# Attention outputs copied whole by ScalarE, shifted by DMA and added on GpSimd; keys loaded in column halves

## The reference, cut to what matters

```python
mod = jax.nn.silu(c) @ w_ada + b_ada                       # shift, scale, gate
h = rmsnorm(x, norm_in) * (1.0 + scale[:, None, :]) + shift[:, None, :]
proj = h @ w_in
# per block of 128 queries: index scores pick 256 keys, then
logits = jnp.einsum('bqhd,bqkhd->bqhk', q_b, k_sel) * att_scale
p = jax.nn.softmax(jnp.where(valid, logits, -jnp.inf), axis=-1)
y_attn = jnp.einsum('bqhk,bqkhd->bqhd', p, v_sel)
y_attn = group_rmsnorm(y_attn, gn_attn, N_HEADS) * jax.nn.silu(az)
y = jnp.concatenate([y_conv, y_attn], axis=-1) @ w_out
return rmsnorm(x + gate[:, None, :] * y, norm_f)
```

## Time and profile before

| | |
|---|---|
| Time, median of 3 runs | 688.26 us (688.07 to 688.32) |
| Profiled execution | 688.04 us |
| Its span | 686.2 us |
| PE busy | 654.1 us, 95% |
| DVE busy | 452.2 us, 66% |
| ACT busy | 376.3 us, 55% |
| POOL busy | 229.4 us, 33% |
| Granted TensorE clock | 0.999 of full speed |

### The profile page before, as it was taken

The page is one execution under the profiler, slowest core; times in us unless marked ns, Lnnn a source line. Parts: engine busy times, 40 slices in busy tenths (PEclk is TensorE's granted clock), DMA queues, the critical chain, the costliest instruction groups (busy, mean ns, idle before and its releaser), DMA issues.

```text
span 686.2 us, 8973 instructions
## 1 busy us (share of the span) xinstructions
PE 654.1 (95%) x3203; PEld 547.5 (80%) x3203; DVE 452.2 (66%) x750; ACT 376.3 (55%) x546; POOL 229.4 (33%) x121
## 2 busy tenths in 40 slices
PE   0999999999999999999999999999999999999996
PEld 0889987878888888888888888788788887778884
DVE  4884746767889999996038750003899898577625
ACT  6766444656562232454552453444899999874202
POOL 1001234343334152657645856540026432000000
PEclk9999999999999999999999999999999999999999
DMA  8960496453333011111010361034884551222431
GB/s 314 381 234 1 140 183 138 137 155 94 93 92 122 33 54 40 57 35 61 32 63 31 123 215 61 32 91 94 281 193 112 124 124 39 87 92 97 150 123 61
DMA packets 27911, 78.64 MB, mean 115 GB/s; under 512 B 3986, under 2 KB 8410, under 8 KB 27868
## 3 DMA queue, kind: packets, MB, share of 16 engines
q1 hardware_dynamic: 27524, 77.03, 37.4%
q10 hardware_dynamic: 344, 1.05, 0.6%
HBM read 61.25 MB, written 13.41 MB: 109 GB/s over the span
## 4 chain that ended last, share of the span: by engine, by line
PE 81%; DVE 5%; DMA 4%; ACT 4%; issue 2%; SPq 1%; POOL 1%; ACTq 1%; DVEq 0%; POOLq 0%
PE ps L808 15%; PE ps L810 15%; PE ps L809 15%; PE ps L1018 4%; PE ps L1020 4%; PE ps L1019 4%; PE ps L845 4%; PE ps L878 2%; PE ps L879 2%; PE ps L966 2%; PE ps L965 2%; PE ps L897 2%; PE ps L898 2%; DMA iqs<-hlL 1%; PE ps L698 1%
## 5 line engine op out<-in xcount | busy, mean ns | idle before, releaser
L808 PE MATMUL ps<-hH,wH 128*128 128x512 f32 (+1 forms) x544 | 211.7, 389 | 0.1
L809 PE MATMUL ps<-hL,wH 128*128 128x512 f32 (+1 forms) x544 | 210.1, 386 | 0.0
L810 PE MATMUL ps<-hH,wL 128*128 128x512 f32 (+1 forms) x544 | 210.1, 386 | 0.0
L1857 POOL TENSOR_TENSOR wL<-raw,wH 128x1024 fp32r<-128x1024 f32 x35 | 87.7, 2505 | 183.8 <-ACT wH L1076 175.7
L810 PEld LDWEIGHTS ps<-hH,wL 128*128 128x128 f32 x544 | 102.1, 188 | 20.3
L808 PEld LDWEIGHTS ps<-hH,wH 128*128 128x128 f32 x544 | 102.1, 188 | 20.1 <-issue 1.6
L809 PEld LDWEIGHTS ps<-hL,wH 128*128 128x128 f32 x544 | 102.2, 188 | 18.5
L1278 ACT ACTIVATE relu<-ps,wabs 128x384 f32<-128x384 f32 (+5 forms) x48 | 40.1, 850 | 39.4 <-PE ps L898 14.6
L1581 DVE SCALAR_TENSOR_TENSOR score<-relu,wsgn,score 128x384 f32<-128x384 f32 (+5 forms) x42 | 49.7, 1183 | 13.6 <-ACT relu L1278 10.2
L1602 DVE TENSOR_SCALAR_CACHE_REDUCE above<-score,srch 128x384 bf16<-128x384 f32 (+5 forms) x60 | 56.8, 946 | 2.1
L1697 DVE TENSOR_TENSOR phL<-ps,phH 128x512 fp32r<-128x512 f32 (+1 forms) x80 | 49.3, 632 | 11.6 <-ACT phH L1234 10.7
(11 more groups left out here) (233 smaller groups left out, 1182.2 us busy)
## 6 DMA issues: line engine op xcount, KB each, us to landing
raw<-in_w_units SPq DMA_DIRECT2D x36, 512.0 KB, 3.4
ks<-qk_halves SPq DMA_DIRECT2D x32, 256.0 KB, 5.9
xin<-in_x SPq DMA_DIRECT2D x8, 512.0 KB, 8.0
wa<-in_w_ada SPq DMA_DIRECT2D x8, 512.0 KB, 11.7
wa<-in_w_ada SPq DMA_DIRECT2D x16, 256.0 KB, 7.7
gw<-in_w_ada SPq DMA_DIRECT2D x8, 512.0 KB, 4.1
qs<-qk_halves SPq DMA_DIRECT2D x16, 256.0 KB, 4.2
wo<-in_w_out SPq DMA_DIRECT2D x8, 512.0 KB, 7.7
```

Source lines behind the costliest of these rows:

```text
L808: pe.matmul(out, wH[slot(n)][:, kt, :], hH[:, kt, cols], start=(kt == 0), stop=False)
L809: pe.matmul(out, wH[slot(n)][:, kt, :], hL[:, kt, cols], start=False, stop=False)
L810: mm = pe.matmul(out, wL[slot(n)][:, kt, :], hH[:, kt, cols], start=False, stop=(kt == KT - 1))
L1857: g.tensor_tensor(wL[slot(n)][:], raw[slot(n)][:], wH[slot(n)][:].bitcast(F32), ALU.subtract).then_inc(s_wL, 1)
```

## The change

**Opening.** Tile 1 joins `STAGED`, so only tile 0 is read from PSUM, and the third unit's first matmul no longer waits for `xT` of tile 1.

**Outputs.** For g below `SHIFTED` = 14, ACT copies the whole bank of 128x512, for an even head into its place in `ya`, for an odd one into the new tile `obuf`. The bank is free from then (`out_read` waits for `s_tmp`). SP shifts the half that lies in the wrong rows to `tmp` with a DMA (`shift_out`), and GpSimd adds (`join`). The last head (g = 14, 15) stays as it was.

**Key loads.** `load_head` loads a head in two halves of 512 columns, six DMAs of 64x512 each, with a semaphore for each half; the shifts, the weight rows (four at head 0, two at head 2) and the denominators (heads 1, 3, 5) stand between them. Head 0 and 1 are loaded in four such parts.

**Tables.** New places for logits, maxima, exponentials, outputs, denominators and group sums. One weight row is split by GpSimd in each of the second and third pair, two in the first.

```diff
-STAGED = (2, 3, 4, 5, 6, 7)
+STAGED = (2, 3, 4, 5, 6, 1, 7)
-LOGITS_AT = (1, 3, 10, 13, 14, 15, 16, 18)
-MAX_AT = (1, 2, 9, 14, 14, 15, 15, 18)
-EXP_AT = (9, 13, 13, 16, 16, 17, 19, 21)
+LOGITS_AT = (2, 5, 5, 11, 16, 16, 18, 20)
+MAX_AT = (0, 4, 6, 10, 15, 16, 17, 20)
+EXP_AT = (6, 9, 15, 18, 18, 19, 21, 24)
-TMP_AT, OUT_AT = 5, 5
+TMP_AT, OUT_AT = 4, 5
+SHIFTED = 2 * (NH - 1)
...
+        def kept_out(g):
+            h, sb = g // 2, g % 2
+            return ya[:, h // 2, HALF * sb:HALF * sb + HALF] if h % 2 == 0 else obuf[:]
...
-                        if n:
-                            pe.wait_ge(s_h, n)
+                        if n == 1:
+                            pe.wait_ge(s_h, 1)
...
+            def shift_out(g):
+                sp.wait_ge(s_tmp, g + 1)
+                if g:
+                    sp.wait_ge(s_join, g)
+                r, d = rows(g // 2), rows(g // 2 + 1)
+                sp.dma_start(tmp[r, :], kept_out(g)[d, :]).then_inc(s_shift, 16)
...
-                if g >= 1:
-                    act.wait_ge(s_o, g)
-                A(tmp[r, :], ps[d, 6 + sb, :], ACT.Copy).then_inc(s_tmp, 1)
+                if g < SHIFTED:
+                    if h % 2 and g > 2:
+                        act.wait_ge(s_join, g if sb else g - 2)
+                    A(kept_out(g), ps[:, 6 + sb, :], ACT.Copy).then_inc(s_tmp, 1)
...
-                    if x in OUTS:
+                    if x in OUTS and OUTS[x] >= SHIFTED:
                         head_out(OUTS[x])
...
+            def join(g_):
+                h, sb = g_ // 2, g_ % 2
+                r = rows(h)
+                pool.wait_ge(s_shift, 16 * (g_ + 1))
+                ...
+                g.tensor_tensor(ya[r, h // 2, HALF * sb:HALF * sb + HALF], kept_out(g_)[r, :], tmp[r, :],
+                                ALU.add).then_inc(s_join, 1)
```

More of the change, by code:

```diff
@@ L193 @@
 HEAD = 2 * STEPS
[L194 to L197, removed]
+DSQ_AT = {HEAD * (2 * t + 1) + (4 if t < NT - 1 else 5): t for t in range(NT)}
+DENS_AT = {HEAD * (2 * t + 1) + (9 if t < NT - 1 else 7): t for t in range(NT)}
+KEEP_AT = {HEAD * (2 * t + 1) + (14 if t < NT - 1 else 9): t for t in range(NT)}
+SUMS_AT = {HEAD * (2 * t + 2) + 7 + 8 * half: (t, half) for t in range(NT - 1) for half in range(2)}
 SUMS_AT[LAST + 15] = (NT - 1, 0)
-KEEP_SUMS_AT = {HEAD * (2 * t + 2) + 5 + 8 * half: (t, half) for t in range(NT - 1) for half in range(2)}
+KEEP_SUMS_AT = {HEAD * (2 * t + 2) + 7 + 9 * half: (t, half) for t in range(NT - 1) for half in range(2)}
 OUT_HIGH_AT = {LAST + x: 4 + n for n, x in enumerate((11, 14, 17, 18))}
@@ L330, in build @@
         tmp = at("tmp", [P, HALF], F32, 76)
+        obuf = at("obuf", [P, HALF], F32, 12)
         masked = [at(f"masked{i}", [P, S], F32, kb) for i, kb in enumerate((56, 60))]
@@ L392, in build @@
         s_wo = sem("s_wo"); s_woH = sem("s_woH"); s_woL = sem("s_woL"); s_woLd = sem("s_woLd")
-        s_stack = [sem(f"s_stack{i}") for i in range(2)]
+        s_stack = [sem(f"s_stack{part}") for part in range(2)]
         s_vh = sem("s_vh"); s_vv = sem("s_vv")
@@ L644, in spread_den, with load_head @@
                                  dd[t, NB * e:NB * e + NB, :].rearrange("(o b) n -> o (b n)", o=1).broadcast_to([HD, S])).then_inc(s_din, 16)
-            for h in range(NH):
-                if h == 2:
+            def load_head(h, part):
+                if h == 2 and part == 0:
                     sp.wait_ge(s_unit, NU)
-                if h >= 2:
+                if h >= 2 and part == 0:
                     sp.wait_ge(s_lg, NB * (h - 1))
+                if h:
+                    sp.wait_ge(s_stack[part], 96 * h)
+                cols = slice(HALF * part, HALF * part + HALF)
@@ new lines, in shift_out @@
+            def shift_out(g):
[4 more added lines that the diff above has]
+                sp.dma_start(tmp[r, :], kept_out(g)[d, :]).then_inc(s_shift, 16)
+            for h in range(2):
+                for part in range(2):
+                    load_head(h, part)
+            for h in range(NH):
+                if h:
+                    shift_out(2 * h - 1)
+                if h + 2 < NH:
+                    load_head(h + 2, 0)
+                if h == 0:
+                    load_head(2, 1)
+                if h < NH - 1:
+                    shift_out(2 * h)
+                if h == 0:
+                    for ct in range(4):
+                        sp.dma_start(wo[:, ct, :], a["w_out"][P * ct:P * ct + P, :]).then_inc(s_wo, 16)
+                elif h + 2 < NH:
+                    load_head(h + 2, 1)
@@ L656, in _ @@
                 if h == 2:
-                    for ct in range(KT - 2):
+                    sp.wait_ge(s_wo, 16 * 4)
+                    for ct in range(4, KT - 2):
                         sp.dma_start(wo[:, ct, :], a["w_out"][P * ct:P * ct + P, :]).then_inc(s_wo, 16)
-                if h >= 3 and h % 2:
-                    spread_den((h - 3) // 2)
+                if h % 2 and h < NH - 1:
+                    spread_den(h // 2)
             sp.wait_ge(s_exp, NB * NH)
@@ L1298, in other_half @@
                 act.wait_ge(s_pv, last_chunk(g) + 1)
[L1299 to L1301 removed]
+                if g < SHIFTED:
+                    if h % 2 and g > 2:
+                        act.wait_ge(s_join, g if sb else g - 2)
+                    A(kept_out(g), ps[:, 6 + sb, :], ACT.Copy).then_inc(s_tmp, 1)
+                else:
+                    act.wait_ge(s_join, SHIFTED)
+                    if sb:
+                        act.wait_ge(s_o, 1)
+                    A(tmp[r, :], ps[d, 6 + sb, :], ACT.Copy).then_inc(s_tmp, 1)
             def pair_cols(t, half):
@@ L1943, in pair_add @@
                 pool.wait_ge(s_sums, 2 * t + half + 1)
+                if half == 0:
+                    pool.wait_ge(s_join, 4 * t + 5)
                 pool.wait_ge(s_din, 32 * (t + 1))
```

62 lines of the change are left out of this document (45 added, 17 removed).

## The result

The changed kernel is slower: median 690.97 us (22 runs; 21 lie between 687.66 and 693.51, and the one of 1344.12 us is left out of the ratio) against 688.03 us for the kernel before (22 runs, 686.76 to 689.39). The ratio is 1.0049, 95% interval 1.0041 to 1.0057. I had forecast 686.4 and a range that ended at 689.9. The profiled execution took 693.33 (span 691.4), 2.4 us above the median, so its losses are larger than the typical ones.

A forecast was written before the change was run, and what follows sets the result against it. TensorE, busy 95% of the span, was taken as the bound. Attention stalls of -2.75 us and new waits of +0.9 gave net -1.85, from the median of 688.26 to 686.4 us; range 684.5 to 689.9.

The forecast's parts named there:

- The step that failed: Attention outputs: next shift, group sums and ACT wait for the join; ACT's loop 8.4 us against 9.7, so no wait.
- The landing: Output shift by DMA: lands between 0 and 5.9 us after issue, the upper bound taken from a 256 KB key load.
- VectorE's relief, -2.75: Attention: 14 output adds leave VectorE, 2.7 us less per pair; TensorE stalls shrink by 1.7, 0.3 and 0.75 us.
- Last exponential, +0.9 in heads 1 to 6: Turn of values block 3: a 2.76 us chain against 2.6 of TensorE work, so 0.15 us wait per head.
- VectorE and GpSimd: Attention: VectorE reads PSUM and one SBUF tile, so it is not open to blocking by GpSimd's SBUF reads.
- Opening, 0: Opening: TensorE's 1.69 us wait for tile 1 goes, but it then waits for VectorE's sums; 0, bounds 0 and -1.8.
- GpSimd's join 1.3: Attention outputs: GpSimd's 64x512 add takes 1.3 us, bounds 0.65 and 1.3; no room problem on GpSimd.
- ACT's whole copy 0.59: Attention outputs: ScalarE's 128x512 copy, 0.59 us, replaces a 64x512 one of 0.592; cost 0.
- key halves: Key loads in halves: 6.5 instead of 3.2 us of SP per head; cost 0, bounds 0 and +1.
- tail 0: End of attention: 8.0 us of TensorE work and 1.85 of stalls, before 6.75 and 1.87; 0, bounds -0.5 and +1.

The follow-up runs named there:

- The shift first: Changed kernel with all three denominator broadcasts issued behind the shift of the odd head's second half, not ahead of it: 687.22 us, ratio 0.9989 to the kernel before.
- VectorE's version: Changed kernel with each odd head's second-half output copied across by ScalarE and added by VectorE, as before: 687.34 us, ratio 0.9992; timed again 686.61, 0.9989.
- the kernel with only the first spread moved: Changed kernel with only the first of three denominator broadcasts moved behind the shift (head 2): 695.85 us, ratio 1.0122 to the kernel before.
- the best profile: First profile of the changed kernel with odd heads' second-half outputs added by VectorE: attention stage 100.2 us, against 101.9 in the kernel before.

## Why the prediction was wrong

- **The step that failed.** "Who waits for it: the next shift, the group sums, and ACT". I named the sums and priced only ACT: 9.7 us of window against a loop of 8.4. The sums' wait stands in my sum at nothing, without a reason. Theirs is the longer chain, with a square (1.04) behind the join, up to 9.4, and the shorter window: counted as I counted ACT's it is 11 of a head's 20 places, 7.6 us, and it measured 6.05. That is up to 1.8 us by my own numbers, and up to 3.4 by the measured window, in each of three heads, slower where I said faster. The runs showed 4.1 us of such waits (2.7, 0.7, 0.7). The shift first and VectorE's version show that this chain is all of the loss.
- **The landing.** The bound of 5.9 us held in the changed kernel (2.2 at least, 2.8 in the middle, 5.4 at most; 6.1 once in the kernel with only the first spread moved), and the case of interest, behind two broadcasts of 256 KB, lay at its upper end. The Trainium skill (SBUF — State Buffer, section The DMA setup-cost knee) has a nearly fixed cost of some 2 us per transfer; the shortest landing, 2.2, agrees, and the 5.4 shows what came on top of it with other transfers in flight. "No wait even at the upper bound, if SP is free": SP was free but for 0.28 us at most, the transfers' engines were not (share 0.98; 0.67 and 0.56 where the same shift took 3.6 us in heads 4 and 6).
- **The clock.** No term for it. It cost 1.7 us in one profile of the changed kernel and none in the other.
- **VectorE's relief, -2.75.** Right in kind: no wait for `ya` is left, and PE's brackets fell from 3.7 to 2.2 us with the shift first. In size it was near: with the shift first the stage shortened by 0.7 (101.9 to 101.2) although it holds 1.0 of waits for the last exponential and 0.6 for a square (0.42 and its 0.16), so the relief was worth 2.3; in the best profile it was 1.7 + 1.0 = 2.7. What is left of it in the medians, net, is 0.4 to 0.8. VectorE's busy time fell by 1.6 to 2.0 us in a full pair, not by 2.7. The new tables and the relief are one edit, not two: with the tables alone it is +5.2.
- **Last exponential, +0.9 in heads 1 to 6.** Right: 6 x 0.16 = 1.0, with the bracket at 0.0 as named, and the chain from the logits' end to that turn took 2.7 us (506.86 to 509.56 in head 2), as worked out (2.76). In the tail the wait of 0.8 came, within a sum of stalls like that of before, as worked out (0.82, 0.19, 0.47).
- **VectorE and GpSimd.** "DVE's work in attention reads PSUM and one SBUF tile and is not open to it" is wrong for `dsq`: beside GpSimd it took up to 1.26 us in the changed kernel and 2.17 in its variants, instead of 0.16. I had no term for it.
- **Opening, 0.** Right, 1.0000, and both successors named are the ones that came (0.64 for `hL`, 0.79 for the sums).
- **GpSimd's join 1.3, ACT's whole copy 0.59, key halves, tail 0.** Right: 1.27 to 1.30, 0.58 to 0.60, no wait for `qs` or `ks`, and from the first output step to the end 102.6 us both times (686.2 - 583.6; 691.4 - 588.8).

## What to carry to other kernels

When a result takes a longer way, list every reader and give each its own window, taken on the engine that reads; the reader with the shortest window decides, and here it was not the one that I had priced. An in-order DMA queue is part of the way: what stands just ahead of the shift sets its landing, and a move in the queue for one head shifts the next. Moved for one of three heads it cost 4 to 5 us more, moved for all three it took the loss away. Parts of a change that were fitted to each other must be tried together; here the tables and the outputs each lose alone.

## What the runs showed of the hardware

- After both stalls of 2.71 us the granted clock of a TensorE that had been busy fell to 0.62 and 0.64 over the next 4.5 us, with DMA traffic and without, and after the one of 5.09 to 0.62; after stalls of 0.43 to 1.78 us (0.43, 1.45, 1.47, 1.53, 1.70, 1.71, 1.78) it stayed at 1.00. Each fall cost some 1.7 us.
- An addition of 64x512 on GpSimd takes 1.28 us, that of 128x512 1.28: half the partitions saves nothing.
- A 128 KB shift within SBUF landed in 2.2 to 5.4 us from its issue in the changed kernel: 5.39 behind two broadcasts of 256 KB, 2.21 in the same place with these behind it.
- A VectorE product of 128x16 out of SBUF took 0.16 to 0.17 us alone, and up to 2.17 when GpSimd was at work on SBUF as it began; it then ended with GpSimd's instruction.
